# One fused decoder forward pass on one core: activation squares moved ahead of the first weight slabs, the last norm's mean subtraction moved to GpSimd

## The reference, cut to what matters

```python
def rmsnorm(x, g):
    xf = x.astype(jnp.float32)
    var = jnp.mean(xf * xf, axis=-1, keepdims=True)
    return (xf * lax.rsqrt(var + RMS_EPS)).astype(x.dtype) * g

def layer_norm(x, g, b):
    xf = x.astype(jnp.float32)
    mu = jnp.mean(xf, axis=-1, keepdims=True)
    var = jnp.mean(jnp.square(xf - mu), axis=-1, keepdims=True)
    y = (xf - mu) * lax.rsqrt(var + LN_EPS) * g.astype(jnp.float32) + b.astype(jnp.float32)
    return y.astype(x.dtype)
```

## Time and profile before

| | us |
|---|---|
| median of 3 runs | 3498.36 |
| lowest, highest run | 3497.62, 3506.7 |
| the profiled execution's own time | 3509.21 |
| its span, first to last instruction | 3507.4 |
| outside the span | 1.8 |
| PE busy in the span | 3210.2 (92%) |
| POOL, DVE, ACT busy | 1388.5, 1206.7, 1112.5 |
| mean granted TensorE clock, of full | 0.961 |

### The profile page before, as it was taken

One profiled execution on the slowest core, in us unless ns is written; L12 is line 12 of the kernel. 1 busy time (PEld: TensorE's weight loads), 2 busy tenths in 40 slices (PEclk: granted clock), 3 DMA queues, 4 the chain that ended last, 5 costly groups with the idle time before them and its releaser, 6 DMA issues.

```text
span 3507.4 us, 58978 instructions
## 1 busy us (share of the span) xinstructions
PE 3210.2 (92%) x24262; PEld 2899.5 (83%) x24262; DVE 1206.7 (34%) x2087; ACT 1112.5 (32%) x1855; POOL 1388.5 (40%) x671
## 2 busy tenths in 40 slices
PE   5998988999998999989789889999899987899997
PEld 5986577987567999989348779999899985789997
DVE  2435643345554211040864151110411056351103
ACT  3223533222543222132343332221422233342222
POOL 4443034443114444444205434444444443254442
PEclk9999999999999999999889999999999998999999
DMA  4211012212002222222002312222222331122221
GB/s 164 73 58 57 1 48 91 85 49 73 13 25 74 84 96 96 95 77 90 7 1 90 114 49 95 90 97 91 72 96 97 101 114 48 61 74 98 97 96 54
DMA packets 72088, 262.17 MB, mean 75 GB/s; under 512 B 7920, under 2 KB 8560, under 8 KB 70800
## 3 DMA queue, kind: packets, MB, share of 16 engines
q1 hardware_dynamic: 70048, 250.32, 21.1%
q10 hardware_dynamic: 1904, 9.94, 0.8%
HBM read 258.13 MB, written 2.10 MB: 74 GB/s over the span
## 4 chain that ended last, share of the span: by engine, by line
PE 84%; DVE 11%; ACT 3%; issue 2%; POOL 0%; DMA 0%; SPq 0%; DVEq 0%; ACTq 0%; POOLq 0%
PE bank L476 23%; PE bank L478 23%; PE bank L480 23%; PE bank L768 2%; PE bank L794 2%; PE bank L759 1%; PE bank L599 1%; DVE s L1482 1%; PE bank L942 1%; ACT wh L1006 1%; PE bank L562 1%; PE bank L650 1%; DVE small L1712 1%; PE bank L641 1%; PE bank L933 1%
## 5 line engine op out<-in xcount | busy, mean ns | idle before, releaser
L341 POOL TENSOR_TENSOR wl<-raw,wh 128x1024 fp32r<-128x1024 f32 x464 | 1154.0, 2501 | 1969.7 <-ACT wh L1006 1969.5
L476 PE MATMUL bank<-xh,wh 128*128 128x256 f32 x5120 | 1030.5, 283 | 79.1 <-POOL xl L355 57.6
L478 PE MATMUL bank<-xl,wh 128*128 128x256 f32 x5120 | 1015.0, 280 | 0.0
L480 PE MATMUL bank<-xh,wl 128*128 128x256 f32 x5120 | 1014.7, 280 | 0.0
L476 PEld LDWEIGHTS bank<-xh,wh 128*128 128x128 f32 x5120 | 788.6, 191 | 105.7 <-issue 105.2
L1006 ACT CAST wh<-raw 128x1024 fp32r<-128x1024 f32 x464 | 471.2, 1047 | 1129.2 <-PE bank L480 1085.2
L480 PEld LDWEIGHTS bank<-xh,wl 128*128 128x128 f32 x5120 | 787.2, 191 | 0.0
L478 PEld LDWEIGHTS bank<-xl,wh 128*128 128x128 f32 x5120 | 786.9, 191 | 0.0
L476 PE MATMUL bank<-hh,wh 128*128 (+1 forms) x1408 | 281.0, 281 | 5.8 <-ACT sg L1313 5.8
L480 PE MATMUL bank<-hh,wl 128*128 (+1 forms) x1408 | 281.0, 281 | 0.0
L478 PE MATMUL bank<-hl,wh 128*128 (+1 forms) x1408 | 280.5, 281 | 0.0
(11 more groups left out here) (314 smaller groups left out, 3519.7 us busy)
## 6 DMA issues: line engine op xcount, KB each, us to landing
raw<-in_slabs SPq DMA_DIRECT2D x464, 512.0 KB, 3.2
h<-in_x_t SPq DMA_DIRECT2D x1, 2048.0 KB, 8.4
w1v<-in_w ACTq DMA_DIRECT2D x2, 1024.0 KB, 4.8
side<-in_pp_w ACTq DMA_DIRECT2D x2, 1024.0 KB, 4.8
xm<-in_mem_t ACTq DMA_DIRECT2D x2, 1024.0 KB, 4.8
out<-h SPq DMA_DIRECT2D x8, 256.0 KB, 2.0
side<-in_w SPq DMA_DIRECT2D x1, 1024.0 KB, 14.2
vt<-in_p_t ACTq DMA_DIRECT2D x2, 512.0 KB, 5.8
```

The source lines that it names most:

```text
L341: nc.gpsimd.tensor_tensor(wl[:, n % RING, :], raw[:, n % RING, :], wh[:, n % RING, :], A.subtract).then_inc(w_low, 1)
L476: nc.tensor.matmul(dst[:, c], high_l, high_r[:, c], start=first and n == 0, stop=False)
L478: nc.tensor.matmul(dst[:, c], high_l, low_r[:, c], start=False, stop=False)
L480: out = nc.tensor.matmul(dst[:, c], low_l, high_r[:, c], start=False, stop=last and n == len(parts) - 1)
```

## The change

It has two parts. At the start, `x` comes by eight transfers of one chunk (256 KB), each with a semaphore of its own, ahead of everything on SP's queue; `cst`, `tb` and `prm` are issued by ACT on its own queue; ACT then squares each chunk as it lands, and casts the first four slabs after the eight squares. DVE waits for `loaded`, now three transfers. In the last norm, DVE copies the mean out of PSUM into `s1`, POOL subtracts it from chunks 1 to 7 of `h` in place, and DVE only scales those chunks.

```diff
@@ SP
-            for ap, src in ((h[:], x_t.rearrange("(c p) t -> p c t", p=P)), (prm[:, 0:NPRM1], prm1),
-                            (cst[:], consts), (tb[:, 0, 0:P], causal)):
-                sp.dma_start(ap, src).then_inc(loaded, 16)
+            for c in range(KC):
+                sp.dma_start(h[:, c, :], x_t[c * P:(c + 1) * P, :]).then_inc(x_in[c], 16)
@@ POOL
+            def centre_last(st):
+                pool.wait_ge(mean_kept, 1)
+                pool.wait_ge(S["stat"], st["stat"] + 2)
+                for c in range(1, KC):
+                    nc.gpsimd.tensor_tensor(h[:, c, :], h[:, c, :], s1, A.subtract).then_inc(centred, 1)
...
+                elif st is stages[-1]:
+                    centre_last(st)
@@ ACT
             def sumsq(st):
                 for c in range(KC):
+                    act.wait_ge(x_in[c], 16)
                     if c >= 2:
                         act.wait_ge(S["s2"], st["s2"] + c - 1)
                     nc.scalar.activation(sq[:, c % 2, :], h[:, c, :], F.Square).then_inc(S["sq"], 1)
...
-            act.wait_ge(loaded, 16 * 4)
+            for ap, src in ((cst[:], consts), (tb[:, 0, 0:P], causal), (prm[:, 0:NPRM1], prm1)):
+                act.dma_start(ap, src).then_inc(loaded, 16)
+            sumsq(stages[0])
             for n in range(RING):
                 high(n)
             act.wait_ge(consts_made, 3)
...
-            for st in stages:
+            for st in stages[1:]:
@@ DVE
                     dve.wait_ge(S["act_stat"], st["act_stat"] + 1)
+                    if last_one:
+                        V.tensor_copy(s1, b_mean).then_inc(mean_kept, 1)
                     dve.wait_ge(S["stat"], st["stat"] + 2)
...
-                        if c:
+                        if c and last_one:
+                            dve.wait_ge(centred, c)
+                        elif c:
                             step(V.tensor_tensor(sg[:, c % 2, :], h[:, c, :], b_mean, A.subtract))
...
-                        src = sg[:, c % 2, :]
+                        src = h[:, c, :] if last_one and c else sg[:, c % 2, :]
...
-            dve.wait_ge(loaded, 16 * 4)
+            dve.wait_ge(loaded, 16 * 3)
```

More of the change, by code:

```diff
@@ L305, in program @@
         consts_made, final, stored, w1k_in = sem("consts_made"), sem("final"), sem("stored"), sem("w1k_in")
+        x_in = [sem(f"x_in{c}") for c in range(KC)]
+        mean_kept, centred = sem("mean_kept"), sem("centred")
         S = {k: sem("s_" + k) for k in total if k not in ("slab", "prod", "took")}
@@ L1446, in _ @@
             act.wait_ge(consts_made, 3)
-            does = dict(sumsq=sumsq, rms=norm, ln=norm, split=split, front=front, nsa=nsa, w_out=w_out, pg=pg, ffn_in=ffn_in,
+            does = dict(rms=norm, ln=norm, split=split, front=front, nsa=nsa, w_out=w_out, pg=pg, ffn_in=ffn_in,
                         ffn_out=ffn_out, da_prep=da_prep, da_project=da_project, da=da, da_norm=da_norm,
                         xa_project=xa_project, xa=xa, pool=pool_mix, xa_rest=xa_rest)
-            for st in stages:
+            for st in stages[1:]:
                 if st["kind"] in does:
```

## The result

Twenty runs of each kernel were made in turn on one chip. Before: median 3509.79 us (3491.81 to 3526.47). Changed: median 3487.07 us (3470.69 to 3513.59). The ratio is 0.9944, with a 95% interval of 0.9924 to 0.9965: 19.7 us saved, between 12 and 27. (The two medians by themselves lie 22.7 apart.) The forecast was 19.0 (ratio 0.9946). The three runs of the kernel before that were known at the forecast are the first three of these twenty. The profiled execution of the changed kernel took 3500.85, its span 3499.1.

What follows compares the result with a forecast made beforehand. PE, busy 92% of the span, was taken to bound the kernel, so only its idle start and end could pay. 15.0 + 4.3 - 0.3 = 19.0 us saved, 3498.4 to 3479.4; range 3476 to 3489.

Steps and rivals of the forecast that it cites:

- the term of 3 us "for what medians move": Whole kernel: 3 us allowed below the best bounds for movement of medians, setting the range's low end at 3476.
- Step 1: Start, loads of x: slabs issued some 2 us later, covered by full transfer engines; slab 0 still at 12.08.
- Step 2: Start, arrivals: last byte ahead of slab 0 at 10.77, constants at 5 to 6, DVE ready to add from 7.
- Rival B: Start: constants land last, at 10.8, holding squares and casts; total gain 14.1, time 3484.3 us, chance 0.11.
- Step 3: Start, squares: 0.6 each, additions 0.70, hidden under arrivals; last square ends at 11.4, PE's means at 16.5.
- Step 4: Start, ACT's casts: 12.1 to 16.8, then a table load; root at 18.1, first `xh` at 22.4.
- Step 5: Start, POOL's low parts: from 13.2, 2.40 each; first `xl` at 22.8, not 37.77; front gain 15.0 us.
- Step 7: Last norm: POOL's seven subtractions 1.29 each, DVE's scalings 0.77; ACT's last addition at 3500.0, not 3504.26; gain 4.3 us.
- rival C: Last norm: POOL and DVE block each other, scalings cost 1.40, no tail gain; 15.0 saved, 3483.4 us, chance 0.08.
- Step 8: Last norm, writing out: 256 KB every 0.77 us barely fits the transfer engines; costs 0.3 us, bounds 0 and 1.0.
- Rival A: Start: x's eight transfers don't flow together; smaller front gain, 9.7 or 4.7; time 3484.7 to 3489.7 us, chance 0.06.
- Rival D: PE's lower clock lasts through its first-stage work; 40 us at that level give 3511.4 us, slower; chance 0.02.

Runs made afterwards that it cites:

- e10: The kernel before, unedited, profiled a second time: front 39.00, middle 3440.74, tail 17.86 us.
- e2: The kernel before with only the last norm's change: median 3507.70 us against 3508.70, ratio 0.9999.
- e1: The changed kernel with the last norm taken back, so the start's change alone: median 3497.34 us against 3508.70, ratio 0.9966.
- e9: The changed kernel, unedited, profiled a second time: front 24.64, middle 3447.50, tail 14.26 us.
- e5: The changed kernel, but DVE adds the squares before it waits for the constants: PE's first product at 23.16 us, executed once.
- e3: The kernel before, loads kept, but ACT squares ahead of the four casts: PE's first product at 28.54 us, executed once.
- e4: The kernel before with the new loads only, casts still ahead of the squares: PE's first product at 37.77 us, executed once.
- e7: The changed kernel with additions ahead of the constants, the fourth slab's cast and low part later, three output buffers: median 3496.02 us against 3514.43, ratio 0.9945.
- e8: The changed kernel, but x in one transfer, still alone on SP's queue: PE's first product at 28.83 us, executed once.

## Why the prediction was right or wrong

**Right: where the time goes.** Front and tail come to 18.0 us in the first pair of profiles. Against the means of all like profiles (fronts of before, e10 and e2 against changed, e1 and e9: 38.86 - 24.70; tails of five against five without the third buffer: 17.88 - 14.28) it is 14.2 + 3.6 = 17.8. I had 15.0 + 4.3 - 0.3 = 19.0.

**Wrong: the range's low side, the term of 3 us "for what medians move".** Three runs, the middle one 0.7 above the lowest, were too few to judge the scatter. Twenty runs of the kernel before reach from 3491.81 to 3526.47. The changed median is 22.7 us below the one before from the same runs; the range, told against 3498.36, allowed 22.4 at most. Set against the runs taken beside it, the changed median is thus a little past the low end; in absolute microseconds it is inside the range only because the median of the twenty runs of before is 11.4 above that of the three. In place of the 3 us, the interval of 12 to 27 us has 7 to either side of its 19.7. It contains the forecast of 19.0 and the 17.8 of front and tail, so scatter is enough to explain the rest; whether part of it is a change of the middle stays open. That 19.7 came so near to 19.0 is in part luck, as front and tail fell 1.2 short of the forecast. I should have given the low side as much room as the high side, where I had counted 8 us.

By the steps of the forecast:

- *Step 1, covered issues:* right. Slab 0 landed at 11.4, not at 12.1; the eight issues took 3.82, the slabs were issued from 4.62.
- *Step 2, constants at 5 to 6:* mis-sized. They landed at 6.97, and DVE could add from 7.98 on. Rival B had the mechanism (the constants late, squares held, casts queued behind), at 10.8 in place of 7.0.
- *Step 3, last square at 11.4:* 13.2, for that reason, as e5 shows (10.9 without the wait). The additions at 0.69 beside no POOL work: right, and e3 against e4 shows that POOL's low parts are what makes them slow. The quicker additions are about half of the order's gain (an estimate, see e3).
- *Step 4, root at 18.1:* 18.95, since PE's means began later.
- *Step 5, first low part at 13.2, each 2.40, first `xl` at 22.8:* 14.17, 2.32 each, 23.4. Of the late start of 1.0 the quicker low parts took back only a part; the 0.6 that is left is what the front fell short of the forecast (14.4 for 15.0). That POOL is the last to be ready: right, though ACT's path was level with it, as e7 showed when POOL's was shortened.
- *Step 6, the copy:* free, with 0.33 to spare.
- *Step 7, subtractions of 1.29 and scalings at 0.77:* 1.27 with no contention, so rival C is out; but the seven scalings took 5.85 and not 5.39. With two output buffers DVE waits 0.20 for ACT every second time, which my "two buffers allow just that" had left out; 0.27 ahead of the last one is put down to no wait ("issue"). The gain up to ACT's last addition is 14.77 - 10.95 = 3.8, not 4.3; e7's third buffer gets most of it back.
- *Step 8, writing out:* from ACT's last addition to the end of the span it is 3.36 where it was 3.14, so 0.2 was lost against the 0.3 that I took.
- *Rival A:* out. The eight pieces landed 3.8 to 5.9 after their issue, flowing together, and with one transfer the front is 4.0 us longer (e8). The Trainium skill, DMA: Bandwidth & Descriptors, section Bandwidth, has the rule to batch to 1 MiB or more. Here it would have misled: the pieces of 256 KB together kept the engines at least as full as the one of 2 MB (busy share from 4 to 10 us 1.06 to 1.07 against 0.92 to 1.06), and ACT could start on the first of them.
- *Rival D, the clock:* not seen. The mean granted clock was 0.961 before and 0.962 changed; after PE's first product the lower level lasted about 3 us in both (an estimate from a clock of 0.70 in 41 to 43 us before and of 0.82 in 27 to 30 changed). But its suspicion that later stages can take another length by themselves was nearer to the truth than I knew.
- *The chances:* the 0.92 is the forecast, B and C; with the half of A that the sentence names it would be 0.95. The 7 subtractions end at 3498.5 by their own numbers, not 3498.6. Neither bears on the forecast.

## What to carry to other kernels

An addition on VectorE with both inputs in SBUF took up to 2.72 us here beside GpSimd's subtractions and 0.69 without them: try an order in which the short chain runs before GpSimd starts, even if the long chain begins later for it. A wait at the head of an engine's program holds everything behind it; check that the first instruction behind it needs what it waits for. And before giving a range, look at how one kernel scatters, part by part: here two pieces of the span repeat within 0.2 to 0.8 us and the third scatters by 21.

## What the runs showed of the hardware that I had not expected

PE's long loops run at one of two paces, in every version. Stretches of 20 us of the same loop, kernel before, then changed (us, busy of PE, PEld, DVE, ACT, POOL with the count of instructions, granted clock, DMA share, GB/s):

```profile
3200.00:3220.00 20.00, 20.00 (x179) 20.00 (x178) 3.60 (x4) 6.01 (x8) 8.66 (x5) 1.00 0.29 100
```

```profile
3200.00:3220.00 20.00, 20.00 (x172) 20.00 (x171) 2.79 (x3) 5.84 (x8) 7.81 (x4) 1.00 0.30 103
```

PE is busy throughout and the granted clock is full in both, but 179 against 172 matmuls start: 111.7 or 116.3 ns each. In all profiles of the table, a feed-forward stage's first loop (some 220 us) has one pace from end to end and its second loop (some 110 us) again one of the two; nearly all its 20 us stretches count 178 or 179, or else 172 or 173. The slow pace costs about 9 us in the first loop and 4.5 in the second, which gives the four lengths of the table, near 378, 382.5, 387.5 and 391.5. Both paces come in every kernel, and the lengths differ between two executions of the same one. As e9 and e10 ran on different chips, the profiles alone don't show whether the pace changes from chip to chip or from execution to execution; but on one chip the run times of the kernel before lie up to 35 us apart. This pace is a part of the scatter of the middle (3440.7 to 3461.7): the three stages of the table add up to 1135 to 1162, and the rest of the middle, 2293 to 2313, scatters too. What sets the pace when a loop is entered was not tried and stays open.
